# Running the second layer's query-side work on tokens 12 to 527 instead of all 528

## The reference

```python
def conv_ffn(h, w_up, conv_w, conv_b, w_down):
    Tp = h.shape[1]
    u = h @ w_up
    up = jnp.pad(u, ((0, 0), (CONV_W - 1, 0), (0, 0)))      # CONV_W = 3
    c = conv_b + sum(up[:, j:j + Tp] * conv_w[j] for j in range(CONV_W))
    gate, val = jnp.split(c, 2, axis=-1)
    return (jax.nn.silu(gate) * val) @ w_down
...
    h = h + diff_attention(rms_norm(h, ln_attn_g[i]), ...)
    h = h + conv_ffn(rms_norm(h, ln_ffn_g[i]), ...)
    return h[:, N_META:T]                                   # N_META = 16, T = 528
```

## Time and profile before

| | |
|---|---|
| median of 3 executions | 2361.52 us (2360.99 to 2362.99) |
| the profiled execution | 2362.81 us, its span 2361.5 us |
| mean granted TensorE clock | 0.972 of full |
| PE / PEld / DVE / ACT / POOL busy | 94% / 82% / 62% / 40% / 20% of the span |
| second layer, from its first `b_q` unit to the last matmul | from 1653.4 to 2358.6 us |

### The profile page before, as it was taken

One profiled execution on the slowest core, in us unless ns is written; L12 is line 12 of the kernel. 1 busy time (PEld: TensorE's weight loads), 2 busy tenths in 40 slices (PEclk: granted clock), 3 DMA queues, 4 the chain that ended last, 5 costly groups with the idle time before them and its releaser, 6 DMA issues.

```text
span 2361.5 us, 44695 instructions
## 1 busy us (share of the span) xinstructions
PE 2215.4 (94%) x19538; PEld 1947.2 (82%) x19538; DVE 1462.9 (62%) x2338; ACT 938.0 (40%) x1590; POOL 462.2 (20%) x277
## 2 busy tenths in 40 slices
PE   4898999999997999987998999999999999999999
PEld 1677777777766787976888999999988889999987
DVE  3687888888867443496556666633355556777722
ACT  1324434344332434433544444322456655444411
POOL 0344343344310344423231000000000011000000
PEclk7899999999998999997999999999999999999999
DMA  6541011111115324310013223223311013223231
GB/s 237 128 111 55 11 42 42 42 42 42 42 60 173 107 90 126 118 38 10 21 37 112 90 90 91 91 92 94 109 45 37 21 36 115 90 90 90 86 107 67
DMA packets 60290, 184.75 MB, mean 78 GB/s; under 512 B 7200, under 2 KB 11296, under 8 KB 60096
## 3 DMA queue, kind: packets, MB, share of 16 engines
q1 hardware_dynamic: 60096, 181.90, 24.9%
HBM read 174.99 MB, written 6.88 MB: 77 GB/s over the span
## 4 chain that ended last, share of the span: by engine, by line
PE 74%; DVE 16%; ACT 5%; issue 2%; DMA 1%; POOL 0%; SPq 0%; DVEq 0%; ACTq 0%
PE PS L540 59%; PE PS L670 4%; DVE ca L1874 3%; PE PS L1025 2%; PE PS L1152 1%; PE PS L865 1%; PE PS L1120 1%; DVE Swk L2273 1%; DVE mx L2269 1%; DVE kx L1942 1%; PE PS L998 1%; DVE Bf L1948 1%; DMA xt<-in_xT 1%; ACT Lb L1200 1%; DVE acc L1804 1%
## 5 line engine op out<-in xcount | busy, mean ns | idle before, releaser
L2560 POOL TENSOR_TENSOR wlo<-raw,whi 128x1024 fp32r<-128x1024 f32 (+2 forms) x154 | 310.4, 2017 | 926.5 <-ACT whi L1200 921.1
L540 PE MATMUL PS<-nhi,whi 128*128 128x264 f32 x2064 | 440.1, 294 | 12.5 <-DVE nlo L2115 6.9
L540 PE MATMUL PS<-nlo,whi 128*128 128x264 f32 x2064 | 423.1, 287 | 0.0
L540 PE MATMUL PS<-nhi,wlo 128*128 128x264 f32 x2064 | 420.4, 285 | 0.0
L1200 ACT ACTIVATE whi<-raw 128x1024 fp32r<-128x1024 f32 (+3 forms) x322 | 306.4, 953 | 226.4 <-PE PS L540 199.4
L540 PEld LDWEIGHTS PS<-nhi,whi 128*128 128x128 f32 x2064 | 324.0, 191 | 22.1 <-DVE qB L2157 5.6
L540 PEld LDWEIGHTS PS<-nlo,whi 128*128 128x128 f32 x2064 | 324.6, 190 | 0.0
L540 PEld LDWEIGHTS PS<-nhi,wlo 128*128 128x128 f32 x2064 | 324.0, 191 | 0.0
L1786 DVE TENSOR_TENSOR wlo<-raw,whi 128x1024 fp32r<-128x1024 f32 (+1 forms) x168 | 201.1, 1197 | 171.9 <-ACT whi L1200 171.6
L540 PE MATMUL PS<-hhi,whi 128*128 128x512 f32 x648 | 264.5, 408 | 7.4 <-DVE hlo L1853 7.3
L540 PE MATMUL PS<-hhi,wlo 128*128 128x512 f32 x648 | 258.4, 399 | 1.6 <-POOL wlo L2560 1.6
(11 more groups left out here) (351 smaller groups left out, 3533.8 us busy)
## 6 DMA issues: line engine op xcount, KB each, us to landing
raw<-in_wall SPq DMA_DIRECT2D x282, 512.0 KB, 3.6
raw<-in_wall SPq DMA_DIRECT2D x16, 384.0 KB, 3.1
TZ<-g_rows SPq DMA_DIRECT2D x2, 2112.0 KB, 8.4
raw<-in_wall SPq DMA_DIRECT2D x32, 128.0 KB, 2.0
raw<-in_wall SPq DMA_DIRECT2D x16, 256.0 KB, 2.6
g_rows<-gsb SPq DMA_DIRECT2D x8, 328.0 KB
xt<-in_xT SPq DMA_DIRECT2D x1, 2048.0 KB, 13.8
o_rows<-os SPq DMA_DIRECT2D x8, 256.0 KB, 2.2
```

What stands on the lines that cost most here:

```text
L540: q = e.matmul(out, cuts[a][:, k * P:(k + 1) * P], (hi_, lo_)[b][:, kr, lo:lo + w], start=start and k == 0 and a == b == 0, stop=stop and ...
L2560: e.tensor_tensor(wlo[slot[i]][:, w], raw[i % NRAW][:, w], whi[slot[i]][:, w].bitcast(F32), ALU.subtract).then_inc(*up("lo_pool", i))
```

## The change

A constant `LATE = 516` is added: tokens 12 to 527. The second layer's queries, their norms, the way out of its attention, the residual addition after it, the operand and statistics made from it, and the `up1` products are done for 516 columns, as two halves of 258 that start at columns 12 and 270. Its meta query block shrinks from 16 rows (tokens 0 to 15) to 4 (tokens 12 to 15). The taps, gate and split of `up1` are done for 512 columns (tokens 16 on) instead of 528. Keys and values, the first layer, and `down1` keep their sizes. No instruction, transfer or wait is added or taken away; all of these keep their order.

```diff
+LATE = 516
...
-        def halves(n, b):
+        def halves(n, b, first=0):
+
             if n <= 512:
-                return [(PS[:, b, 0:n], 0, n)]
-            return [(PS[:, b, 0:HT], 0, HT), (PS[:, b + 1, 0:HT], HT, HT)]
+                return [(PS[:, b, 0:n], first, n)]
+            return [(PS[:, b + p, 0:n // 2], first + p * n // 2, n // 2) for p in range(2)]
...
-        def rows_of(i):
-            return (0, 16, 16) if i == 4 else (16 + P * i, P, WIDTH[i])
+        def rows_of(i, first=0):
+            return (first, 16 - first, 16) if i == 4 else (16 + P * i, P, WIDTH[i])
+
+        def late_rows(i):
+            return rows_of(i, T - LATE)
...
-                    sums(sqh, T, 4, mat).then_inc(*up(name + "_sum", k))
+                    sums(sqh, LATE, 4, mat).then_inc(*up(name + "_sum", k))
...
-                        normed(f"up{layer}", ("U", layer, j, n), (lambda k: on.wait_ge(*at(rhs, k))) if j == n == 0 else None)
-                residual(f"down{layer}", f"ffn{layer}", fhi[layer], flo[layer], f"f{layer}", 3, last=layer == 1)
+                        normed(f"up{layer}", ("U", layer, j, n), (lambda k: on.wait_ge(*at(rhs, k))) if j == n == 0 else None,
+                               (T, LATE)[layer])
+                residual(f"down{layer}", f"ffn{layer}", fhi[layer], flo[layer], f"f{layer}", (T, S)[layer], 3)
...
-                normed("b_q", ("qb_raw", h), (lambda k: on.wait_ge(*at("ffn0_n", k))) if h == 0 else None)
+                normed("b_q", ("qb_raw", h), (lambda k: on.wait_ge(*at("ffn0_n", k))) if h == 0 else None, LATE)
...
-                        sums(sqb, T, 4, ones).then_inc(*up("ob_sum", h))
+                        sums(sqb, LATE, 4, ones).then_inc(*up("ob_sum", h))
...
-            residual("b_out", "res_b", ohi_b, olo_b, "ob", first=4)
+            residual("b_out", "res_b", ohi_b, olo_b, "ob", LATE, first=4)
...
-                    act(nhi[:, j, :], H[:, j, :], ACT.Copy, scale=col(gname, gj + j)).then_inc(*up(name + "_hi", j))
+                    act(nhi[:, j, c:], H[:, j, c:], ACT.Copy, scale=col(gname, gj + j)).then_inc(*up(name + "_hi", j))
...
-                        evac(U0[layer][n][:, 2:2 + T], b, i, "U", layer, j, n)
+                        evac(U0[layer][n][:, 2 + T - (T, LATE)[layer]:2 + T], b, i, "U", layer, j, n, n=(T, LATE)[layer])
...
-                    e.tensor_tensor(V2[1], V2[0], V2[1], ALU.mult).then_inc(*up("f_gated", layer, j))
+                    e.tensor_tensor(V2[1][:, c:], V2[0][:, c:], V2[1][:, c:], ALU.mult).then_inc(*up("f_gated", layer, j))
```

More of the change, by code:

```diff
@@ L863, in sums, with normed @@
             def sums(src, n, b, mat):
-                for out, lo, w in halves(n, b):
+                for out, lo, w in halves(n, b, T - n):
                     q = e.matmul(out, mat, src[:, lo:lo + w], start=True, stop=True)
                 return q
-            def normed(what, then, rhs=None):
+            def normed(what, then, rhs=None, n=T):
                 b = pair_of_banks(then)
-                full(what, nhi, nlo, halves(T, b), rhs)
+                full(what, nhi, nlo, halves(n, b, T - n), rhs)
                 flush()
@@ L901, in tensor, with steps_of @@
             later.append(first_stats)
-            def steps_of(what, b, hi_, lo_, rhs=None, k0=0):
-                for k, _ in enumerate(product(what, hi_, lo_, halves(T, b), rhs, k0=k0)):
+            def steps_of(what, b, hi_, lo_, rhs=None, k0=0, n=T):
+                for k, _ in enumerate(product(what, hi_, lo_, halves(n, b, T - n), rhs, k0=k0)):
                     if k == {"a_in": 5, "b_kv": 3, "a_out": 0, "b_out": 1}[what]:
@@ L1041, in tensor, with residual @@
             run(SELECT, a=attend_a(), s=select(), d=nothing(), r=nothing(), g=made_a())
-            def residual(what, name, hi_, lo_, rhs, n_units=1, last=False, first=0):
+            def residual(what, name, hi_, lo_, rhs, n, n_units=1, first=0):
                 for j in range(8):
@@ L1046, in residual @@
                     for c in range(n_units):
-                        full(what, hi_, lo_, [(PS[:, b, 0:S], 16, S)] if last else halves(T, b),
-                             (lambda k: on.wait_ge(*at(rhs, k))) if j == 0 else None,
+                        full(what, hi_, lo_, halves(n, b, T - n), (lambda k: on.wait_ge(*at(rhs, k))) if j == 0 else None,
                              start=(c == 0), stop=(c == n_units - 1), k0=first + 8 * c)
-                if not last:
-                    norm_end(name)
+                if n > S:
+                    norm_end(name, n)
             def ffn(layer, rhs):
@@ L1090, in made_beside @@
                     b = pair_of_banks(("res_b1", j))
-                    yield from steps_of("b_out", b, ohi_b, olo_b, (lambda k: on.wait_ge(*at("ob", k))) if j == 0 else None)
+                    yield from steps_of("b_out", b, ohi_b, olo_b, (lambda k: on.wait_ge(*at("ob", k))) if j == 0 else None, n=LATE)
                     yield
@@ L1602, in scalar, with residual @@
             a_last = max(i for i in range(NU) if units[i][0] == "a_in")
-            def residual(what, name, gname, gj, n_units, last=False):
+            def residual(what, name, gname, gj, n, n_units):
+                c = T - n
                 for j in range(8):
@@ L1607, in residual @@
                         passed()
-                    if last:
+                    if n == S:
                         continue
@@ L2353, in vector, with residual @@
             run(SELECT, a=attend_a(), s=nothing(), d=select(), r=rounds(), g=made_a())
-            def residual(name, gname, gj, n_units, last=False, after=None):
-                n, c0 = (S, 16) if last else (T, 0)
+            def residual(name, gname, gj, n, n_units, after=None):
+                c0, last = T - n, n == S
                 def rest(j):
                     on.wait_ge(*at(name + "_hi", j))
-                    operand_lo(j, col(gname, gj + j), name + "_n")
+                    operand_lo(j, col(gname, gj + j), name + "_n", c0)
                     on.wait_ge(*at(name + "_sq", j))
-                    accumulate(j, sq[:, j % 2, :], acc[:, 0:T], name + "_squares")
+                    accumulate(j, sq[:, j % 2, c0:], acc[:, c0:T], name + "_squares")
                 for j in range(8):
@@ L2377, in ffn @@
             def ffn(layer, gname=None, gj=0):
+                c = 16 * layer
                 for j in range(22):
@@ L2394, in ffn @@
                     on.wait_ge(*at("taps", layer, j, 1))
-                    e.tensor_tensor(V2[1], V2[0], V2[1], ALU.mult).then_inc(*up("f_gated", layer, j))
+                    e.tensor_tensor(V2[1][:, c:], V2[0][:, c:], V2[1][:, c:], ALU.mult).then_inc(*up("f_gated", layer, j))
                     on.wait_ge(*at("f_hi", layer, j))
-                    e.tensor_tensor(flo[layer][:, j, :], V2[1], fhi[layer][:, j, :].bitcast(F32),
+                    e.tensor_tensor(flo[layer][:, j, c:], V2[1][:, c:], fhi[layer][:, j, c:].bitcast(F32),
                                     ALU.subtract).then_inc(*up(f"f{layer}", j))
-                residual(f"ffn{layer}", gname, gj, 3, last=gname is None)
-            residual("res_a", "ln_ffn_g_2", 0, 1, after=("res_a1", 2))
+                residual(f"ffn{layer}", gname, gj, (T, S)[layer], 3)
+            residual("res_a", "ln_ffn_g_2", 0, T, 1, after=("res_a1", 2))
             ffn(0, "ln_attn_g_2", 8)
@@ L2542, in vector @@
             run("g" * 16 + 8 * BESIDE + AFTER, a=attend(), g=made_beside())
-            residual("res_b", "ln_ffn_g_2", 8, 1, after=("res_b1",))
+            residual("res_b", "ln_ffn_g_2", 8, LATE, 1, after=("res_b1",))
             ffn(1)
```

113 lines of the change are left out of this document (59 added, 54 removed).

## The result

The changed kernel took 2356.81 us (median of 22 executions, 2353.53 to 2360.25), the kernel before 2361.22 (median of 22) in the same comparison: a ratio of 0.9983, 95% interval 0.9976 to 0.9990. It became faster by 4.4 us. The forecast was 7.7 us. The time lies inside the forecast range, near its upper end; the sign is right and the size is not. At 0.17% the gain is, by its middle, inside the 0.2% that the prediction called hardly distinguishable from nothing: the case that it gave a chance of 0.10, and not the faster one that it gave 0.83.

What follows compares the result with a forecast made beforehand. The prediction took TensorE's matmuls to bound most of the second layer, VectorE and ScalarE the residual rounds. Its terms, 5.57 + 1.04 + 0.34 + 0.39 + 0.37 + 0.04 = 7.75 us, gave 2353.8 us, range 2351.5 to 2357.5.

Steps and rivals of the forecast that it cites:

- What bounds the kernel: TensorE bounds `up1`, `down1` and `b_q`; from 1953.3 to 1984.8 a VectorE and ScalarE round of 2.92 us equals TensorE's half unit.
- What a column costs: Slope between `up1` at 264 and `down1` at 512 columns: 0.449 ns a column, 2.70 ns a matmul for six.
- The term of `up1`: In `up1` from its second unit on, 2064 matmuls each save 2.70 ns, all on the chain: 5.57 us.
- that of `b_q`: In the second layer's query products, 384 matmuls each save 2.70 ns, on the chain: 1.04 us.
- The rival of the starting bytes: Reads starting off a 32-byte boundary cost more and the kernel gets slower, 2383.6 us; chance 0.07.
- The weight load as a floor: The weight load sets the pace at 264 columns, shorter matmuls gain nothing: 2360.8 us; chance 0.09 together with coarse column steps.
- The gap of columns over 2.4 GHz plus 2.5 ns: The skill's warm matmul gap: 112.5 ns where 121.5 is measured; its slope would make the sum about 0.5 us smaller.
- `sums`: 17 `sums` in TensorE's queue (queries, attention, residual), each 0.020 us shorter for 12 columns: 0.34 us.
- Attention and `b_out` beside it: `b_out`, heads 0 to 3: 143 matmuls beside the attention save 0.39 us; stage forecasts, with `sums`, 0.14 and 0.21 us.
- Residual stage: `b_out`, heads 4 to 7, with the addition: VectorE and ScalarE's round decides, 46 ns shorter, eight rounds, 0.37 us.
- The clock: Half clock after idle stretches, at the first matmuls of `b_q` and `b_kv`: one stretch more or less, 1.4 us either way.
- the step from queries to keys: From 1708 to 1714, where TensorE waits through ScalarE and VectorE: four instructions in line 12 columns shorter, 0.04 us.

Runs made afterwards that it cites:

- the 520 tokens: The changed kernel with four tokens more, 8 to 527, as two halves of 260 from columns 8 and 268: 2354.88 us, ratio 0.9975.
- the 260 and 256: The changed kernel with its 516 columns cut into 260 from column 12 and 256 from column 272: 2354.09 us, ratio 0.9974; again 2354.10, ratio 0.9972.
- the dear start first: The changed kernel with nhi and nlo moved by 8 bytes, so column 270 falls on a boundary and column 12 does not: 2365.54 us, ratio 1.002.
- the move by 16 bytes: The kernel before with nhi and nlo moved by 16 bytes, both halves starting 16 bytes past a 32-byte boundary: 2359.78 us, ratio 0.9995.
- two pieces of 256: The changed kernel with `up1` products alone as 256 columns from 16 and 256 from 272, zeros for tokens 12 to 15: one execution, 2353.63 us.
- the two cuts with all starts on a boundary: The changed kernel cut into 260 and 256 columns (2354.10 us, ratio 0.9972), or 256 from column 12 and 260 from column 268 (2354.09, 0.9970).
- 524 tokens: The changed kernel with tokens 4 to 527, halves of 262 from columns 4 and 266, the second 8 past a boundary: 2362.07 us, ratio 1.0007.

## Why the prediction came out as it did

- *What bounds the kernel.* Right for `up1`, which is TensorE's from end to end before and after, and every nanosecond of a matmul showed in the span. Wrong for most rounds of the residual stage, below.
- *What a column costs.* The 2.70 ns for six columns was right as the price of columns: 3.3 to 3.6 ns for eight was measured, 2.5 to 2.7 for six by the same slope. Single widths scatter around that line by up to 0.5 ns a matmul (the 520 tokens lie 0.4 below it, the 260 and 256 0.2 above), and what makes them do so stays open.
- *The term of `up1`, 5.57 us, and that of `b_q`, 1.04.* Here the prediction failed. It took 2.70 ns as the change of the whole matmul. It is the change of its columns, and every second matmul starts 8 bytes past a 16-byte boundary and pays 2.5 ns for it. That leaves 2.70 - 1.25 = 1.45 ns on the mean, 3.0 us in `up1` where 3.14 were measured (1.52 ns), and 0.56 + 0.14 = 0.70 in the `b_q` stage where 0.40 were. With both pieces on boundaries the two stages gained 5.14 and 1.10 us, near the 5.57 and 1.18 forecast. Why `b_q` gained less than 0.70 stays open; the order of the two starts counts there, since a unit and its `sums` took 6.69 us in the changed kernel, 6.63 with the dear start first and 6.60 with none (6.73 before).
- *The rival of the starting bytes*, with a chance of 0.07, was the true mechanism, in part. I had named its place and the price at which it turns the sign, 2.7 ns on every matmul. Its real price is near that, 2.5, but only one start in two is off the boundary, so it took 2.6 of the 5.6 us and left the sign. The step that failed is the evidence against it: I put the boundary at 32 bytes, and cited 132-column matmuls starting 16 bytes past one. Those start on a 16-byte boundary, and the move by 16 bytes shows that this is free for split matmuls too. No row of the trace had a read at 8 bytes past, and the text said so; the bound for it should then have stood in the range of the forecast and not in a rival of 0.07.
- *The weight load as a floor.* This rival did not hold, as the prediction had argued: two pieces of 256 run at 118.2 ns. The Trainium skill, "TensorE: Matmul & The Clock Gate", section "Back-to-back issue gap", says that the load and the matmul set the spacing together. These runs can't confirm that, since the spacing still fell from 264 to 256 columns; a lower bound that no run here reached may still exist.
- *The gap of columns over 2.4 GHz plus 2.5 ns,* from the same section of the Trainium skill, is too short for this stream. The section gives it for a matmul by itself and not for a stream of them. It would make 109.2 ns at 256 columns, where 118.2 is measured, and 2.5 for six columns. Its slope, 0.417, lies at the lower end of the 0.42 to 0.45 measured from 264 to 256; no run tells what the extra 9 ns are.
- *`sums`.* 0.87 for 0.89 us, as forecast. These are plain fp32, and the second half of them starts at column 270 too, with no cost to be seen: averaged over the first seven in `b_q`, from the first of their four matmuls to the product that follows, they took 0.682 us, and 0.684 and 0.679 in the two cuts with all starts on a boundary. A cost of 2.5 ns on two of the four would be 0.005, so one of that size isn't wholly excluded.
- *Attention and `b_out` beside it.* 0.04 and 0.16 us for 0.14 and 0.21. With aligned pieces they gave -0.28 and 0.32. The terms are small, and I did not take them apart: why the attention stage gained nothing stays open.
- *Residual stage.* The 0.37 us came nearly true, 0.33, and partly by luck. The prediction let the round of VectorE and ScalarE decide all eight rounds. Five of them, from the first addition to `H` to the sixth, were TensorE's: it is busy in all of them, and each addition starts 0.03 to 0.04 us after the last matmul of its half unit. The round is 24 matmuls at the kernel's own spacing, 24 x 120.1 = 2.88 us in the changed kernel. Windows over the five rounds of the kernel before, the changed one, the 260 and 256, and 524 tokens:

```profile
1955.10:1969.70 14.60, 14.60 (x122) 14.60 (x121) 10.20 (x16) 8.97 (x15) 6.09 (x6) 1.00 0.47 152
1953.05:1967.48 14.43, 14.43 (x122) 14.43 (x121) 10.02 (x15) 8.86 (x15) 6.08 (x6) 1.00 0.55 154
1954.67:1968.96 14.29, 14.29 (x122) 14.29 (x121) 10.02 (x15) 8.87 (x15) 6.10 (x6) 1.00 0.55 158
1953.55:1968.18 14.63, 14.63 (x122) 14.63 (x121) 10.13 (x16) 8.94 (x15) 6.05 (x6) 1.00 0.50 153
```

  VectorE and ScalarE do the same work in the second and third line, yet the third is 0.14 us shorter; with 524 tokens they do less than before, and the rounds are not shorter. So these five gained 0.17 us, where TensorE's columns alone, 5 x 65 ns, would have given 0.32: here too the start took half. VectorE's own chain is only 0.02 to 0.03 us shorter than the round, so the rows of before hardly told which of the two decides. From the sixth addition to the end of the `sums` the chain does run through VectorE and ScalarE, and it fell from 14.69 to 14.53 us. VectorE's instructions fell by 11 to 13 ns and most of ScalarE's by 8 to 12, for twelve columns, as forecast.
- *The clock.* The two stretches of half clock in the second layer kept their places and lengths (3.4 and 6.8 us, before and after), and the step from queries to keys took 5.61 us for 5.65, as forecast.

## What to carry to other kernels

When a change trims a tile, the price per column is only half of the account: look at the byte at which each piece now starts, and cut the pieces so that each starts on a multiple of 16 bytes, even at the price of unequal widths or of a few columns more (516 tokens as 260 and 256 columns, and 520 tokens, both beat 516 in equal halves here). When two engines seem to take equally long over a round, ask of each what the round becomes if it alone decides. An operand tile can be moved by some bytes with nothing else changed; this one experiment prices the start alone, and 524 tokens, no faster than 528, showed that one start in two off the boundary outweighs two columns of every matmul. Where no row of a trace shows a new address or shape, its cost belongs into the forecast's range from both sides.

## What the hardware showed that I had not expected

For the split matmuls (type fp32r in the rows) of about 260 columns in a dense stream at full clock, the start of the moving read is free at 0 and at 16 bytes past a 32-byte boundary (121.8 and 121.5 ns at 264 columns), costs 2.5 ns at 8 bytes past a 16-byte boundary and 3.6 ns at 4 bytes past. The end of the read did not decide it, nor did the number of 16-byte stretches touched. ScalarE's writes of `nhi` took 738 ns before and 739 with the tile 8 bytes past, VectorE's of `nlo` 767 and 769, so they showed no such cost, and the plain fp32 sums none that stands out of their scatter. A piece that ends one PSUM bank and one that begins the next can be read by VectorE and ScalarE as one stretch of 516 columns, with no cost seen.
